# Attention's first weights fetched and split ahead of their norm, squares taken among the last gate tiles

## The reference

```python
h = h + concat(diff_attention, ssd_mixer, gla_mixer)(rms_norm(h) @ w_in) @ w_out
f = rms_norm(h)
h = h + (silu(f @ w_ffn_gate) * (f @ w_ffn_up)) @ w_ffn_down      # D_FF = 2816
h = h + sigmoid(h @ ple_w_gate) * (p @ ple_w_proj)
```

```python
sh1, sc1, g1, sh2, sc2, g2 = split(silu(c) @ ada_w[i] + ada_b[i], 6)
x = x + g1 * attention(rms_norm(x) * (1 + sc1) + sh1)
x = x + g2 * swiglu(rms_norm(x) * (1 + sc2) + sh2)
```

## Time and profile before

| | us |
|---|---|
| median of three runs | 2336.46 |
| lowest, highest | 2334.03, 2341.03 |
| the profiled execution | 2342.8 |
| its span (first to last instruction) | 2341.0 |
| mean granted TensorE clock | 0.979 |

### The profile page before, as it was taken

One profiled execution on the slowest core, in us unless ns is written; L12 is line 12 of the kernel. 1 busy time (PEld: TensorE's weight loads), 2 busy tenths in 40 slices (PEclk: granted clock), 3 DMA queues, 4 the chain that ended last, 5 costly groups with the idle time before them and its releaser, 6 DMA issues.

```text
span 2341.0 us, 44967 instructions
## 1 busy us (share of the span) xinstructions
PE 2185.9 (93%) x17588; PEld 2075.4 (89%) x17588; DVE 1598.4 (68%) x2655; ACT 1092.3 (47%) x1752; POOL 0.2 (0%) x4
## 2 busy tenths in 40 slices
PE   5889999998899999898999999999988999998998
PEld 4779899987798999898999888999887999897998
DVE  4676587756756877566778766778777854666554
ACT  3545444445454443455444455544465444555443
POOL 0000000000000000000000000000000000000000
PEclk8999999999999999999999999999999999999999
DMA  4464399934653998444599544699543965542664
GB/s 125 107 162 147 104 303 300 292 100 110 166 158 104 302 299 282 117 143 138 189 301 297 184 145 131 215 300 298 169 127 122 291 193 166 144 134 83 191 185 135
DMA packets 545379, 436.40 MB, mean 186 GB/s; under 512 B 27472, under 2 KB 470904, under 8 KB 545144
## 3 DMA queue, kind: packets, MB, share of 16 engines
q1 hardware_dynamic: 541904, 431.21, 60.5%
q10 hardware_dynamic: 3368, 3.71, 0.5%
HBM read 433.82 MB, written 1.05 MB: 186 GB/s over the span
## 4 chain that ended last, share of the span: by engine, by line
PE 80%; DVE 9%; ACT 5%; DMA 2%; DVEq 2%; issue 1%; SPq 1%; ACTq 1%
PE bank L644 12%; PE bank L646 12%; PE bank L645 12%; PE acc L644 7%; PE acc L646 7%; PE acc L645 7%; PE bank L788 3%; PE bank L1160 2%; PE bank L844 2%; ACT w_hi L1284 2%; DVE w_lo L1734 1%; PE bank L654 1%; PE bank L709 1%; PE bank L710 1%; PE bank L713 1%
## 5 line engine op out<-in xcount | busy, mean ns | idle before, releaser
L1284 ACT ACTIVATE w_hi<-wslot 128x1024 fp32r<-128x1024 f32 x590 | 610.5, 1054 | 534.2 <-PE acc L646 253.5
L644 PE MATMUL bank<-h_hi,w_hi 128*128 128x256 f32 x2784 | 792.5, 285 | 27.3 <-DVE w_lo L1734 10.6
L645 PE MATMUL bank<-h_lo,w_hi 128*128 128x256 f32 x2784 | 778.3, 280 | 0.0
L646 PE MATMUL bank<-h_hi,w_lo 128*128 128x256 f32 x2784 | 778.3, 280 | 0.0
L1734 DVE TENSOR_TENSOR w_lo<-wslot,w_hi 128x1024 fp32r<-128x1024 f32 x412 | 494.2, 1221 | 219.4 <-ACT w_hi L1284 218.8
L644 PEld LDWEIGHTS bank<-h_hi,w_hi 128*128 128x128 f32 x2784 | 525.7, 189 | 45.4 <-DVE w_lo L1728 14.1
L645 PEld LDWEIGHTS bank<-h_lo,w_hi 128*128 128x128 f32 x2784 | 529.1, 190 | 2.2 <-issue 1.7
L646 PEld LDWEIGHTS bank<-h_hi,w_lo 128*128 128x128 f32 x2784 | 526.5, 189 | 0.0
L644 PE MATMUL acc<-mid_hi,w_hi 128*128 128x256 f32 x1120 | 317.7, 284 | 7.8 <-DVE mid_lo L2279 4.6
L646 PE MATMUL acc<-mid_hi,w_lo 128*128 128x256 f32 x1120 | 312.6, 279 | 0.0
L645 PE MATMUL acc<-mid_lo,w_hi 128*128 128x256 f32 x1120 | 312.6, 279 | 0.0
(11 more groups left out here) (286 smaller groups left out, 2987.1 us busy)
## 6 DMA issues: line engine op xcount, KB each, us to landing
wslot<-in_ada_w_dram SPq DMA_DIRECT2D x192, 512.0 KB, 5.7
wslot<-in_ffn_w_gate_dram SPq DMA_DIRECT2D x88, 512.0 KB, 4.9
wslot<-in_ffn_w_up_dram SPq DMA_DIRECT2D x88, 512.0 KB, 5.4
wslot<-in_ffn_w_down_dram SPq DMA_DIRECT2D x88, 512.0 KB, 3.7
wslot<-in_w_in_dram SPq DMA_DIRECT2D x72, 512.0 KB, 4.8
wslot<-in_sb_w_in_dram SPq DMA_DIRECT2D x48, 512.0 KB, 4.5
wslot<-in_w_ffn_gate_dram SPq DMA_DIRECT2D x44, 512.0 KB, 4.7
wslot<-in_w_ffn_up_dram SPq DMA_DIRECT2D x44, 512.0 KB, 5.4
```

What stands on the lines that cost most here:

```text
L644: pe.matmul(dst, w_hi[:, w, cols], hi, start=start, stop=False, skip_group_check=True)
L645: pe.matmul(dst, w_hi[:, w, cols], lo, start=False, stop=False, skip_group_check=True)
L646: return pe.matmul(dst, w_lo[:, w, cols], hi, start=False, stop=stop, skip_group_check=True)
L1284: return act.activation(dst, src, ACT.Copy)
```

## The change

Five of the six attention norms are "early" ones: all but the first. Two of these follow a ple phase ("squared"), three follow a feed-forward block of the second stack. Of these three, two are "late" ones: those after a feed-forward block with eleven modulation blocks.

- SP: the loads of a feed-forward block that stood ahead of its last pair (first stack), or the attention's units 0 and 1 that stood in the norm (second stack), are issued after the first pair's loads.
- ACT and DVE: units 0 and 1 are split at the end of the feed-forward block, or among the last gate tiles of ple, and no longer in the norm.
- Squares: in ple, ACT squares pair 0 after tile 3, pair 1 after tile 5, pairs 2 and 3 after tile 7, with the table of the sigmoid loaded; the norm loads the Ln and Exp table after them.
- Late norms: `ada_unit` 2 and 3 of the last modulation block move from the last step of the feed-forward block to the norm, ahead of DVE's wait for the root; `ada_sum` moves to PE's part of the norm, between the sums of squares and `clear_acc`; `ada_store` to DVE's, behind the scaled tiles. PE's first value product waits for `ada_stored`.

```diff
--- before.py
+++ after.py
@@ -189,7 +189,15 @@
             counts.update(w_high=1, **slots(SLOT_MIX + 1, [1]))
-        phase("norm", counts, split=split, **more)
+        prior, kinds = phases[-1][0], [kind for kind, _, _ in phases]
+        early = split == "att" and prior != "setup"
+        late = None
+        if early:
+            was = phases[-1][2] if prior == "ple" else phases[len(kinds) - 1 - kinds[::-1].index("ffn")][2]
+            was.update(att_at=dict(at), att=more["att"], att_layer=more["layer"])
+            if prior != "ple" and ada_blocks(was["ada"]) == ADA_STEPS:
+                late = was["ada"], was["start"]
+        phase("norm", counts, split=split, early=early, late=late, squared=prior == "ple", **more)
 
@@ -216,7 +224,7 @@
         start = dict(at)
-        phase("ffn", counts, ada=ada, **more)
+        phase("ffn", counts, ada=ada, start=start, att=None, **more)
         add(gate=None if more["stack"] == 1 else (more["layer"], 5), last=("down_done", 0))
@@ -503,6 +511,14 @@
 
+            def first_load(kind, l, n, used):
+                w, _, offs = att_weights(kind, l)
+                need = used.get(f"slot{n}", 0) + 1
+                if kind == "swa" and n:
+                    kv_load(w, n, 0, need)
+                else:
+                    load(n, mix_slot(n), unit(w, KT, offs[n]), need)
+
             def ffn_weights(stack, l):
@@ -524,11 +540,8 @@
                     w, _, offs = att_weights(ph["att"], ph["layer"])
-                    for n in range(3):
-                        if ph["att"] == "swa" and n:
-                            kv_load(w, n, 0, u[n] + 1)
-                        else:
-                            load(n, mix_slot(n), unit(w, KT, offs[n]), u[n] + 1)
+                    for n in range(2 if ph["early"] and not ph["squared"] else 0, 3):
+                        first_load(ph["att"], ph["layer"], n, at)
                 elif kind == "att":
@@ -603,6 +616,15 @@
                     two_steps([None, 2 * P], [0, P], [base[n] + n % 2 + n // 4 for n in range(6)], *block(0), a_base)
+                    if ph["stack"] == 1:
+                        ple_unit(0, ph["layer"], ph["next"])
+                        ple_unit(1, ph["layer"], ph["next"])
+                        for n in range(2):
+                            used = ph["next"].get(f"slot{SLOT_PROJ + n}", 0)
+                            load(SLOT_PROJ + n, wslot[:, SLOT_PROJ + n, :], a["ple_w_proj"][ph["layer"]][P * n:P * n + P, :], used + 1)
+                    elif ph["att"]:
+                        for n in range(2):
+                            first_load(ph["att"], ph["att_layer"], n, ph["att_at"])
                     for lo, hi in runs([block(i)[0] for i in range(NF // 2 - 1)], 1):
@@ -615,12 +637,6 @@
                     i = NF // 2 - 1
-                    if ph["stack"] == 1:
-                        ple_unit(0, ph["layer"], ph["next"])
-                        ple_unit(1, ph["layer"], ph["next"])
-                        for n in range(2):
-                            used = ph["next"].get(f"slot{SLOT_PROJ + n}", 0)
-                            load(SLOT_PROJ + n, wslot[:, SLOT_PROJ + n, :], a["ple_w_proj"][ph["layer"]][P * n:P * n + P, :], used + 1)
                     two_steps([(NF - 1) * P, None], [(NF - 2) * P, (NF - 1) * P],
@@ -839,6 +855,8 @@
                         pe.wait_ge(sem["negmax"], g("negmax") + 2 * i)
+                    else:
+                        pe.wait_ge(sem["ada_stored"], g("ada_stored"))
                     for t in range(TT):
@@ -1159,6 +1177,8 @@
                     mm.then_inc(sem["sumsq"], 1)
+                    if ph["late"]:
+                        ada_sum(ph["late"][1], ADA_STEPS - 1)
                     clear_acc()
@@ -1230,7 +1250,7 @@
                     down(NF - 1, 1, PART_LAST, last=True)
-                    if blocks == ADA_STEPS:
+                    if blocks == ADA_STEPS and ph["stack"] == 1:
                         ada_sum(at, blocks - 1)
@@ -1318,6 +1338,13 @@
                 copy(w_hi[:, part, :], wslot[:, n, :]).then_inc(sem["w_high"], 1)
+
+            def first_high(kind, n, at):
+                mix_high(n, n, unit_loads(at, kind, n, 0))
+
+            def square_pair(q, ready):
+                act.wait_ge(sem["x_ready"], ready)
+                act.activation(sqT[:, 2 * q:2 * q + 2, :], xT[:, 2 * q:2 * q + 2, :], ACT.Square).then_inc(sem["squares"], 1)
 
@@ -1618,15 +1645,13 @@
                     act.preload_act_table_set(LN_EXP)
-                    if ph["split"] == "att":
-                        for n in range(2):
-                            mix_high(n, n, unit_loads(at, ph["att"], n, 0))
+                    if ph["split"] == "att" and not ph["early"]:
+                        first_high(ph["att"], 0, at)
+                        first_high(ph["att"], 1, at)
                     if ph["split"] == "ffn":
                         high(1, 3, 16 * (g("slot1") + g("extra1") + 1))
-                    for q in range(4):
-                        act.wait_ge(sem["x_ready"], g("x_ready") - 3 + q)
-                        act.activation(sqT[:, 2 * q:2 * q + 2, :], xT[:, 2 * q:2 * q + 2, :], ACT.Square)\
-                           .then_inc(sem["squares"], 1)
+                    for q in range(0 if ph["squared"] else 4):
+                        square_pair(q, g("x_ready") - 3 + q)
                     act.wait_ge(sem["sumsq"], g("sumsq") + 1)
@@ -1682,8 +1707,11 @@
                     step(NF - 1, 1, more=False)
-                    for m in range(2 if ph["stack"] == 1 else 0):
-                        ple_high(m, ph["next"])
+                    for n in range(2):
+                        if ph["stack"] == 1:
+                            ple_high(n, ph["next"])
+                        elif ph["att"]:
+                            first_high(ph["att"], n, ph["att_at"])
                 elif kind == "ple":
@@ -1700,6 +1728,12 @@
                             ple_high(m + 5, at)
+                        if m in (5, 6):
+                            first_high(ph["att"], m - 5, ph["att_at"])
+                        if m in (3, 5):
+                            square_pair(m // 2 - 1, g("x_ready") + m // 2)
+                    for q in (2, 3):
+                        square_pair(q, g("x_ready") + q + 1)
 
@@ -1727,6 +1761,9 @@
                    .then_inc(slot_used[n], 1)
+
+            def first_low(n, at):
+                low_of(n, n, at.get(f"high{n}", 0) + 1)
 
@@ -2178,9 +2215,13 @@
                     w = gain_of(gain)
-                    if ph["split"] == "att":
-                        for n in range(2):
-                            low_of(n, n, g(f"high{n}") + 1)
+                    if ph["split"] == "att" and not ph["early"]:
+                        first_low(0, at)
+                        first_low(1, at)
+                    if ph["late"]:
+                        ada, start = ph["late"]
+                        for n in (2, 3):
+                            ada_unit(start, ada, ADA_STEPS - 1, n, True)
                     if ph["split"] == "ffn":
@@ -2202,6 +2243,8 @@
                             h_low(k - 2)
+                    if ph["late"]:
+                        ada_store(start, ada, ADA_STEPS - 1)
                     if shifted and ph["split"] == "att":
@@ -2291,13 +2334,17 @@
                     for b in range(2):
-                        step(NF - 2 + b, b, NF // 2 - 1, more=b == 0, block=blocks == ADA_STEPS)
-                    for m in range(2 if ph["stack"] == 1 else 0):
-                        low(PLE_SLOTS[m], PLE_PARTS[m], ph["next"]["w_high"] + m + 1)
+                        step(NF - 2 + b, b, NF // 2 - 1, more=b == 0,
+                             block=blocks == ADA_STEPS and (b == 0 or ph["stack"] == 1))
+                    for n in range(2):
+                        if ph["stack"] == 1:
+                            low(PLE_SLOTS[n], PLE_PARTS[n], ph["next"]["w_high"] + n + 1)
+                        elif ph["att"]:
+                            first_low(n, ph["att_at"])
                 elif kind == "modulation":
                     n = ph["ada"]
-                    if ada_blocks(n) == ADA_STEPS:
+                    if n < DEPTH:
                         ada_store(ph["start"], n, ADA_STEPS - 1)
@@ -2324,6 +2371,8 @@
                             ple_low(m + 5)
+                        if m >= 6:
+                            first_low(m - 6, ph["att_at"])
                 elif kind == "store":
...
                     for t in range(TT):
```

## The result

The change makes the kernel slower: 2347.15 us median of 17 runs, beside 2339.81 of 17 runs of the kernel before on the same chips. The ratio is 1.0041, 95% interval 1.0028 to 1.0054, so 9.6 us more (6.6 to 12.6) where 9.0 less was forecast; the medians themselves differ by 7.3. The time lies above the range given. (One of the 17 runs of before took 5501 us; the median does not feel it.)

What follows compares the result with a forecast made beforehand. PE, busy 93% of the span, was taken as the bound. Gains 12.2 + 8.0 + 3.8 + 0.3 = 24.3 less losses 11.9 + 3.4 = 15.3 made 9.0 faster: 2336.5 - 9.0 = 2327.5 us, range 2315 to 2340.

Steps and rivals of the forecast that it cites:

- Ple ends: At two ple ends, squares and splits moved between sigmoids let PE sum without a pause: gain 12.2 us, extremes 8.6 to 13.
- The rival of another table: Squares in ple need another table, so each costs ACT a load before and after: 3.0 us later, 2330.5, chance 0.10.
- Ends of the first stack's blocks: At the ends of two feed-forward blocks, PE's waits behind four loads and a half-clock stretch go: gain 8.0 us, bounds 5 to 8.
- Starts: At five feed-forward block starts, moved loads make gate unit 3 late and PE stalls: loss 11.9 us, 7.7 of it first stack.
- no second stall: At the block starts, units behind gate 3 each have over 1 us to spare, so no further stall was counted.
- The sign set for being wrong: Prediction wrong if the starts' stalls come below 8 or above 20 us, or the ple ends give less than 9.
- Clock: Behind the 3.85 us pauses at block starts, longer than the 2.89 after which the clock fell: two half-clock stretches, loss 3.4 us.
- rivals 3 and 4: One: block starts stall twice, 2345.7, chance 0.13; other: late norms win nothing, their starts at half clock, 2333.9, chance 0.12.
- Rival 3: PE stalls twice at block starts, half clock at all five: 33.5 us lost against 24.3 gained, 2345.7, chance 0.13.
- Late norms: At two norms of the second stack, earlier squares and sums bring first tiles forward: gain 3.8 us, bounds 0 and 7.8.
- Third norm: Second stack: waits for the last down unit go, two low parts delay sums: gain 0.3 us, between -1 and 1.2.
- rival 1: The early loads are hidden in DMA idle time before the first pair's loads, losses vanish: 2312.2, chance 0.13.

Runs made afterwards that it cites:

- the fastest among them: Early loads behind gate and up unit 2, ple part as changed, second stack's high parts early, low parts in the norm, no late norms: 2309.9 us, 0.9881 of before.

## Why the prediction was wrong

**Ple ends: right** in size and in each step, 12.5 for 12.2. The rival of another table is false: the squares at 962.86 and 963.99 have no table load between them and the sigmoid. The page "ScalarE: Activation LUTs" of the Trainium skill, section "Table sets: the hidden batching unit", does not name the square among the functions that every set has; the trace shows no table was loaded for it under the sigmoid's table, and decides against reading from that list that a square needs another.

**Ends of the first stack's blocks: right**, 8.9 and 9.1 for 8.0, though just above the bound of 8; nothing else was late.

**Starts: the step that failed first.** How late gate unit 3 is, by "3.3 - 0.6 = 2.7 late" and "1.05/0.31 + 1.05/0.39 = 6.0 us, less 0.6", came out too small. Gate unit 3 was 6.3, 7.2, 3.8, 3.2 and 4.5 late for 5.4, 5.4, 2.7, 3.5 and 2.7, which is 5.3 us more in sum. Without the 0.6 of spare DMA time the sum would be 3.0 longer, and with rows of 4 KB at 310 GB/s (the 390 taken for them stands in no row; the 408 is of runs of 2 KB) another 1.4; single starts scatter too much to part the two. The spare from landing to need was some 1.35 and not 1.55. The pauses (PE's largest step from start to start, less its usual 0.11) were 5.2, 5.4, 2.3, 2.3 and 3.0: 18.2 for 11.9. The mechanism was right, and so was "no second stall". The sign set for being wrong, stalls below 8 or above 20, did not show: it left out the clock and the norms.

**Clock: the second term.** "So two half-clock stretches, 3.4" took the pause of 2.89 for a border that shorter pauses stay below. Pauses of 2.1 to 5.2 us by the waits were followed by half clock, all five: 7.9 by the experiment with products in the pauses, 4.5 more than counted. This was the clock half of rivals 3 and 4. Rival 3's time, 2345.7, comes near the 2347.15 measured, but by luck: its second stall did not happen and the starts lost 26.6 us, not its 33.5; late norms that lost in the first profile, where it counts 3.8 of gain, and half clock elsewhere filled the difference.

**Late norms: the bound that I set aside held.** I wrote "0, if PE's pause of 1.7 in the middle takes the clock down", took 3.8, and measured -2.6 to +2.4 of gain over two executions. DVE was done at 1322.3, before the 1323.0 forecast, but zeros and warming products took 4.7 us and not 3.0, and the first tiles 6.8 and not 5.5; of these 11.5 us nearly 7 were at half clock. The wait that the sum added stood on PE with everything behind it; put behind the warming products, the same sum gives 7.0 for two norms in its one profile.

**Third norm:** 0.3 forecast, -0.9 and -0.1 measured in the two profiles; with low parts back in the norm 0.0. Two profiles of one kernel differ by as much there, so nothing is shown beyond its being small.

**Where I looked in the wrong place.** I asked whether the new loads hide where they were put (rival 1), read shares near 1 there, and was right that they don't. The question that was worth 26 us is where DMA is idle: 12 us and more, just before, behind the one load whose slot was not yet free.

**What stays open.** The listed stretches sum to +8.7 in one pair of profiles and +3.0 in the other, the spans differ by 4.4 and 10.3, the ratio gives 9.6. So 4.3 less and 7.3 more lie elsewhere. The kernel after has 14 and 17 us more of half clock outside the listed stretches (whole traces: 129.3 and 124.5 us after, 99.7 and 105.4 before), some 7 and 9 us of loss by my estimate, since at half clock PE does half the products (15 against 29 in 3.5 us, above); in the first pair a faster pace in long blocks (last section) gives about as much back. One half-clock stretch of 6.8 us at the end of layer 1's attention in the second stack came in both profiles of after and in neither of before (2.6 and 2.3 us). It came in four of the eight variants too, the fastest among them, and why it falls there is not settled.

## What to carry to other kernels

On an in-order queue, place a prefetch by where the engine behind it is idle, and ahead of the first issue that waits; behind that issue it delays a refill by about its bytes over the rate (here 310 GB/s on average). A wait added to a busy matmul engine costs its own length, and it can cost the clock and so everything queued behind it at that clock (11.0 us in place of 7.3 at a late norm), so work that nobody needs yet goes behind what fills the gap, not ahead. And read the price of a pause from short pauses too before taking the shortest one with half clock for the border.

## What the hardware showed that I had not expected

At a granted clock of 1.00 the same products come at two paces. Windows of 150 us in the last feed-forward block, identical code, of before and of before again:

```profile
2150.00:2300.00 150.00, 149.72 (x1273) 149.55 (x1273) 76.90 (x91) 66.29 (x91) 0.00 (x0) 1.00 0.62 183
```

```profile
2140.00:2290.00 150.00, 149.84 (x1319) 149.66 (x1318) 78.41 (x95) 68.90 (x93) 0.00 (x0) 1.00 0.65 186
```

1273 products against 1319: 0.118 and 0.114 us from start to start, PE busy all the time in both. It made 6.1 us in this block and 4.2 in the one before it, of the 12.9 by which the two profiles of one kernel differ: as much as the change did. Four of the twelve profiles here had the faster pace in the last block (both of after, one of before, and the kernel with the ple part alone). What sets it no run shows. A gain of a few us is therefore to be read from the stretches where the code differs, not from the span of one profile.
